# Splitting the next site's fourth weight unit with GpSimd and VectorE before the joint between two sites

## The reference, cut to what matters

```python
for layer in range(DEPTH):            # DEPTH = 2
    g = norm_gains[layer]
    h = rmsnorm(x, g[0])
    x = x + 0.5 * rmsnorm(swiglu(h, w_ffn_gate[layer, 0], w_ffn_up[layer, 0], w_ffn_down[layer, 0]), g[1])
    h = rmsnorm(x, g[2])
    x = x + rmsnorm(token_mixer(h, w_in[layer], w_out[layer], ...), g[3])
    h = rmsnorm(x, g[4])
    x = x + 0.5 * rmsnorm(swiglu(h, w_ffn_gate[layer, 1], w_ffn_up[layer, 1], w_ffn_down[layer, 1]), g[5])
```

## Time and profile before

| what | value |
|---|---|
| time, median of 3 runs (range) | 1447.91 us (1447.5 to 1447.99) |
| time of the profiled execution | 1447.95 us |
| its span | 1446.1 us |
| busy: PE / PEld | 1410.0 / 1165.4 us |
| busy: DVE / ACT / POOL | 1006.0 / 716.8 / 73.0 us |
| mean granted TensorE clock | 0.999 |

### The profile page before, as it was taken

How to read it: one execution, slowest core, us unless ns; L and a number is a source line. 1 busy time by engine, 2 the same in 40 slices (tenths; PEclk the granted TensorE clock), 3 DMA queues, 4 the chain that set the end, 5 groups by cost and what they waited for, 6 DMA issues and landing times.

```text
span 1446.1 us, 22441 instructions
## 1 busy us (share of the span) xinstructions
PE 1410.0 (97%) x8223; PEld 1165.4 (81%) x8223; DVE 1006.0 (70%) x1669; ACT 716.8 (50%) x1228; POOL 73.0 (5%) x98
## 2 busy tenths in 40 slices
PE   5999999999999999999999999999999999999998
PEld 2768756878848888888978888888888888788887
DVE  2589445359637777787697777777777876877776
ACT  3433255245446444475665444564444756644444
POOL 0300211110100000000110000000000002000000
PEclk9999999999999999999999999999999999999999
DMA  9622166265225655655444655646665644455652
GB/s 333 219 88 87 59 210 216 87 193 167 96 87 189 229 186 194 213 177 146 146 132 148 201 174 176 213 150 202 195 195 191 190 130 134 131 175 174 203 197 94
DMA packets 197943, 243.31 MB, mean 168 GB/s; under 512 B 4560, under 2 KB 179184, under 8 KB 197744
## 3 DMA queue, kind: packets, MB, share of 16 engines
q1 hardware_dynamic: 194560, 229.43, 49.4%
q0 software_dynamic: 2736, 10.82, 2.2%
q10 hardware_dynamic: 576, 2.10, 0.4%
HBM read 241.27 MB, written 1.05 MB: 168 GB/s over the span
## 4 chain that ended last, share of the span: by engine, by line
PE 86%; DMA 5%; DVE 4%; ACT 3%; issue 2%; SPq 0%; POOL 0%; DVEq 0%; ACTq 0%; POOLq 0%
PE bank L1880 41%; PE bank L2388 18%; PE bank L2390 9%; DMA weight_ring<-in_w_ada 2%; PE bank L2284 2%; PE bank L2007 1%; DMA weight_ring<-in_w_ffn_up 1%; ACT weights_high L935 1%; PE bank L1861 1%; DVE weights_low L1476 1%; PE bank L2229 1%; PE bank L2152 1%; DMA weight_ring<-in_w_in 1%; PE bank L2552 1%; PE bank L2191 1%
## 5 line engine op out<-in xcount | busy, mean ns | idle before, releaser
L1476 DVE TENSOR_TENSOR weights_low<-weight_ring,weights_high 128x1024 fp32r<-128x1024 f32 x328 | 393.5, 1223 | 126.6 <-ACT weights_high L935 126.4
L935 ACT ACTIVATE weights_high<-weight_ring 128x1024 fp32r<-128x1024 f32 x328 | 334.5, 1048 | 104.3 <-PE bank L1880 62.1
L2388 PE MATMUL bank<-input_split,weights_high 128*128 128x512 f32 x1280 | 319.5, 391 | 0.0
L2388 PEld LDWEIGHTS bank<-input_split,weights_high 128*128 128x128 f32 x1280 | 234.7, 188 | 44.9
L2390 PEld LDWEIGHTS bank<-input_split,weights_low 128*128 128x128 f32 x1280 | 174.6, 190 | 12.5
L2390 PE MATMUL bank<-input_split,weights_low 128*128 128x256 f32 x1280 | 178.5, 282 | 0.0
L1880 PE MATMUL bank<-weights_high,hidden_high 128*128 128x512 f32 x352 | 138.8, 394 | 1.3 <-DVE hidden_low L1585 1.3
L1880 PE MATMUL bank<-weights_low,hidden_high 128*128 128x512 f32 x352 | 137.9, 392 | 0.0
L1003 ACT ACTIVATE silu_gate<-gate_sum 128x256 f32<-128x256 f32 x88 | 36.8, 418 | 202.3 <-DVE gate_sum L1563 200.2
L1880 PE MATMUL bank<-weights_high,hidden_low 128*128 128x512 f32 x352 | 137.0, 389 | 0.0
L1880 PE MATMUL bank<-input_split,weights_high 128*128 128x256 f32 x576 | 105.6, 285 | 0.0
(11 more groups left out here) (337 smaller groups left out, 2228.4 us busy)
## 6 DMA issues: line engine op xcount, KB each, us to landing
weight_ring<-in_w_ffn_gate SPq DMA_DIRECT2D x44, 1024.0 KB, 5.4
weight_ring<-in_w_ffn_up SPq DMA_DIRECT2D x44, 1024.0 KB, 5.4
weight_ring<-in_w_ffn_down SPq DMA_DIRECT2D x44, 1024.0 KB, 4.9
weight_ring<-in_w_in SPq DMA_DIRECT2D x32, 1024.0 KB, 5.4
weight_ring<-in_w_ada SPq DMA_DIRECT2D x24, 1024.0 KB, 6.9
weight_ring<-in_w_out SPq DMA_DIRECT2D x16, 1024.0 KB, 4.9
weight_ring<-in_w_in SPq DMA_DIRECT2D x24, 512.0 KB, 4.6
gain_row<-in_norm_gains POOLq DMA_DIRECT2D x6, 512.0 KB, 4.0
```

Of the source, the lines that this page charges most:

```text
L935: A(unit_in(WH, U), unit_source(U), ACT.Copy).then_inc(s_high, 1)
L1476: TTn(unit_in(WL, U), unit_source(U), unit_in(WH, U).bitcast(F32), ALU.subtract).then_inc(s_low, 1)
L2388: mm(b[:, :].rearrange("p (h n) -> p h n", h=2), unit_in(WH, U)[:, k, :], HX[:, k, :, :], start=(k == 0), stop=False, skip_group_check=True)
```

## The change

Behind a feed-forward site with a successor, the next site's fourth unit gets its high part by a copy on GpSimd, which waits for the ring slot and for `s_used` to reach the next base - 2. Its low part is made by DVE as the last thing of the site, ahead of `site_tail`. Both are taken out of `site_norm`. As the high part no longer counts on `s_high`, ACT's next high part counts two. The order of the low parts, and so the meaning of `s_low`, stays.

```diff
@@ gpsimd, loop over the sites
+                if i < 5 and kind == "ffn":
+                    early = unit_base[i + 1] + EARLY - 1
+                    pool.wait_ge(*filled(UNITS2[early][0]))
+                    pool.wait_ge(s_used, early - SPLIT + 1)
+                    pool.tensor_copy(unit_in(WH, early), unit_source(early)).then_inc(*done("ob_square", "fourth high", i + 1))
 
                 if i < 5:
                     nxt = i + 1
@@ scalar
-            def high(U, j=None):
+            def high(U, j=None, count=1):
...
-                A(unit_in(WH, U), unit_source(U), ACT.Copy).then_inc(s_high, 1)
+                A(unit_in(WH, U), unit_source(U), ACT.Copy).then_inc(s_high, count)
@@ scalar, site_norm
                     x_square(i, 0, hf)
-                if i and SITES[i - 1][0] == "ffn":
-                    high(unit_base[i] + EARLY - 1)
                 for c in range(KD):
...
-                high(unit_base[i] + 4)
+                high(unit_base[i] + 4, count=2 if i and SITES[i - 1][0] == "ffn" else 1)
@@ vector, site_norm
-                if i and SITES[i - 1][0] == "ffn":
-                    low(unit_base[i] + EARLY - 1)
-
@@ vector, ffn, the end
                 for U in ahead[1:]:
                     low(U)
+                if i < 5:
+                    U = unit_base[i + 1] + EARLY - 1
+                    dve.wait_ge(*at("ob_square", "fourth high", i + 1))
+                    TTn(unit_in(WL, U), unit_source(U), unit_in(WH, U).bitcast(F32), ALU.subtract).then_inc(s_low, 1)
```

## The result

The changed kernel takes 1449.82 us (median of 19 runs, 1448.56 to 1451.22), the kernel before 1447.62 us (19 runs, 1446.42 to 1448.57). The ratio is 1.0017 with a 95% interval of 1.0011 to 1.0024: slower by 1.6 to 3.5 us. The profiled span grows from 1446.1 to 1448.1 us. The forecast change, +3.4 us, was about 1 us too much; another 0.3 us of the forecast time is the starting value, 1447.91 us from 3 runs, now 1447.62 us from 19.

What follows compares the result with a forecast made beforehand. TensorE bounds the kernel, and in the joints it waits for DVE's queue. Three joints at 1.29 us less 0.44 us of gains give +3.4 us on 1447.95 us, forecast 1451.3 us, range 1447.9 to 1453.0 us.

Steps and rivals of the forecast that it cites:

- A joint is as long as DVE's queue: Between sites: TensorE waits for DVE's update, so DVE's queue sets the joint, 4.28 us near 628 us.
- ACT's removed high part: Joint, between ACT's squares and first input chunk: the copy is hidden by update and transposes, so removing it gives 0.
- The removed low part: DVE, ahead of the inverse norm: removal ends TensorE's 0.36 us wait in the first mixer; at most 0.08 us elsewhere.
- The moved low part: DVE, site's end before the first gain product: 1.14 us against 0.85 us slack, costing 0.29 us per joint, +0.87 us.
- The copy takes 1.1 us, of which 1.0 us is held: GpSimd copy beside DVE's three subtractions at the site's end: 1.1 us long, 1.0 us of it put into DVE's queue.
- Taking turns: Site's end: GpSimd's copy and DVE's two-input SBUF subtractions block each other, so the copy's time enters DVE's queue; chance 0.60.
- The chance of 0.60: Given to turn-taking with a copy near 1.1 us: 1450.7 to 1452.2 us, nearly all of it slower.
- The earlier refill: SP refills the fourth unit's slot some 9 us earlier; costed at 0, as TensorE has no wait for weights there.
- No turn-taking: Site's end: the one-input copy runs beside DVE's subtractions unhindered; +0.43 us, 1448.3 us; chance 0.26.
- the slow copy: GpSimd: rounding to fp32r slows the copy to the addition's rate, 2.5 us; +7.9 us, 1455.8 us; chance 0.06.
- The clock: Start of a site: TensorE granted 1.2 instead of 2.4 GHz, +5.8 us for each joint hit; chance 0.03.
- the rival of a faster kernel: Mixers: all 1.6 us of TensorE's waits in both go, without turn-taking; -2.8 us, 1445.1 us; chance 0.03 faster.

Runs made afterwards that it cites:

- The last experiment: Kernel before, with ACT's square-root table load moved earlier and, in mixers, DVE's low part of the fourth unit put behind the inverse norm: 1447.85 us, ratio 1.0005.

## Why the prediction was right, point by point

- **A joint is as long as DVE's queue.** Right for what is put into it: earlier squares on ACT leave the changed joint at 5.39 us, and each 0.84 us put into the queue comes out as some 0.85 us of joint. It doesn't hold for what is taken out: with 0.45 us less on DVE ahead of the update the joint of the kernel before is only 0.16 us shorter.
- **ACT's removed high part gives 0.** Right for this joint: 4.26 us without it, 4.28 with it. But it had no slack left, and costs 0.37 us as soon as DVE is earlier.
- **The removed low part gives 0.36 us in the first mixer and at most 0.08 us in another place, 0.44 in all.** Right in kind, too small: the wait is gone, and back with the low part, but it was worth 0.60 us, because idle time behind overlapping matmuls is shorter than the delay that it stands for. The second mixer, put at nothing because it shows no wait, gives 0.13 us. Together 0.73 us. A gain of 0.08 us near 942 us can't be told from what untouched stretches vary by.
- **The moved low part costs 0.29 us.** 0.23 us, by the run in which GpSimd only writes. Half of the 0.06 us is that TensorE's last down matmul starts 6.03 us behind DVE's first subtraction there (624.70 - 618.67) and 6.00 us in the kernel before (626.07 - 620.07). The other half is on DVE, whose first update there starts 5.94 us behind that subtraction, 0.26 us later than the 5.68 us of the kernel before.
- **The copy takes 1.1 us, of which 1.0 us is held.** The copy: 1.13 us, and 1.04 undisturbed against the 1.10 of the sum, whose 0.1 us of fixed time no row shows. The held part was the term that was mis-sized: 0.84 us. I had taken it from an addition near 430 us, where 1.1 of 1.28 us were held, and had rounded up. The page of the Trainium skill that I had set beside it (GPSIMD Engine Reference, "Performance versus the Vector engine", 1.03 cycles an element) gives an estimate of 0.88 us for the length of the copy; the trace shows 1.04 us, 0.16 more. That 0.88 is near the held 0.84 us is no confirmation, as the page says nothing of the held part. With the measured terms my own sum gives 3 x (0.84 + 0.23) - 0.73 = +2.5 us.
- **Taking turns.** Right, and shown: a reading copy holds 0.84 us, two hold 1.68, a writing fill holds nothing. The rule of the Trainium skill (SBUF — State Buffer, "SBUF: two separate sides") says that a VectorE operation with two SBUF inputs is in the way only of a GpSimd operation that reads SBUF; the fill (3.50 us kept) and the gain products (0.69 us kept) agree with both halves of it. That the whole of the instruction is held comes out a little shorter here: DVE loses 0.84 us to a copy of 1.04.
- **The size of the whole.** Forecast +3.4, measured about +2.2 by the medians, 2.5 by the ratio and 2.5 by the stretches of the trace. Three terms were off, all to the same side: the held part by 0.5 us (3 x 0.16), the low part by 0.2 us (3 x 0.06), the gain in the mixers by 0.3 us (0.73 for 0.44). That is the whole difference. The predicted 5.6 us for a joint became 5.36, and the first gain product came not 1.7 but 1.4 us later (5.40 instead of 3.98 us behind the first of the three subtractions). The chance of 0.60 went to the right mechanism, but to a range that these terms put too high.
- **The earlier refill costs nothing.** Right: SP issues it 9.2 us earlier against the joint (at 1128.00, before at 1136.27, in the last joint), and TensorE's waits inside the mixers are as before (1.6 us). The last experiment shows the other side: 2.2 us later costs the second mixer 1.2 us.
- **Rivals.** No turn-taking fell by the 4.34 us, the slow copy by the 1.13 us: rounding to fp32r costs GpSimd nothing that shows. The clock stayed at its full level. The mixers won 0.73 us, all at the norm's products; the 1.6 us of waits in each that the rival of a faster kernel was after stayed.

## What to carry to other kernels

Before work is moved out of a joint, look up which engine's queue the joint is made of, and how much slack that queue has at the new place: here 0.85 us of slack was asked to hold 1.14 us of subtraction and 0.84 us of waiting for GpSimd, in three joints, to save a copy that was hidden and 0.73 us in two mixers. Look up the second longest path too: shortening DVE's queue by 0.45 us brought only 0.16 us, as ACT's copy came next. And before a step that frees a buffer is moved back, look at the transfer that waits for it. GpSimd is not a free third engine beside a VectorE that subtracts two SBUF tensors: a copy of 1.04 us there cost VectorE 0.84 us. Beside operations with an operand in PSUM (0.69 us kept), or as a fill that reads nothing (3.50 us kept), the same GpSimd time cost VectorE nothing.

## What the runs showed of the hardware that was not expected

GpSimd's copy with rounding to fp32r is fast: 1.04 us for 128x1024 values, against 0.95 us for a fill of the same size and 1.04 us for ScalarE's copy of a unit (median of 328). And a copy that starts 0.23 us before the end of a VectorE subtraction loses only about 0.1 us itself, while the next subtraction loses 0.84 us; a second one that comes when the next subtraction has begun loses 1.92 - 1.04 = 0.88 us.
